# Three later output projections: from one fp32 matmul per chunk to three passes over split operands, weights split in halves

## The reference, cut to what matters

```python
y = jnp.dot(o.reshape(...) * jax.nn.silu(z_x), w_out)      # odd layer: "od_out" in the kernel; x = x + gate * y
x = x + even_mixer_2(rms_norm_2(x, even_norm[i]), ...)      # ends in  o @ w_out            ("e2_out")
x = x + conv_ffn(rms_norm_2(x, ffn_norm[layer]), ...)       # starts with h @ w_up          ("up0", "up1")
x = x + diff_mixer(rms_norm_2(x, odd_norm[i]), ...)         # ends in  o... @ w_out         ("df_out")
```

## Time and profile before

| | |
|---|---|
| median of 3 runs | 2526.52 us (2524.41 to 2529.04) |
| the profiled execution | 2524.14 us, its span 2522.3 us |
| PE busy | 2408.3 us, 95% |
| DVE, ACT, POOL busy | 1147.6, 970.0, 305.8 us (45%, 38%, 12%) |
| DMA | 190.58 MB, mean 76 GB/s |

### The profile page before, as it was taken

How to read it: one execution, slowest core, us unless ns; L and a number is a source line. 1 busy time by engine, 2 the same in 40 slices (tenths; PEclk the granted TensorE clock), 3 DMA queues, 4 the chain that set the end, 5 groups by cost and what they waited for, 6 DMA issues and landing times.

```text
span 2522.3 us, 32773 instructions
## 1 busy us (share of the span) xinstructions
PE 2408.3 (95%) x12528; PEld 1788.9 (71%) x12528; DVE 1147.6 (45%) x1875; ACT 970.0 (38%) x1596; POOL 305.8 (12%) x206
## 2 busy tenths in 40 slices
PE   7999899898999998999999999999999879999998
PEld 4888665466878776665776578888877654888886
DVE  5000454644441106633436356665554452666644
ACT  4111336544254325533325343333342562333423
POOL 2233001200332420000000000004400000000142
PEclk9999799999999999999999999999999999999999
DMA  7122141100231201122220122323322102332331
GB/s 302 53 65 62 67 157 43 58 1 1 74 110 55 80 23 62 51 99 84 77 87 5 42 92 92 98 93 92 100 84 84 42 1 67 96 97 91 93 99 42
DMA packets 51581, 190.58 MB, mean 76 GB/s; under 512 B 5723, under 2 KB 6107, under 8 KB 51196
## 3 DMA queue, kind: packets, MB, share of 16 engines
q1 hardware_dynamic: 51452, 188.78, 23.0%
HBM read 186.66 MB, written 2.10 MB: 75 GB/s over the span
## 4 chain that ended last, share of the span: by engine, by line
PE 89%; ACT 4%; DVE 4%; issue 2%; DMA 0%; POOL 0%; SPq 0%; DVEq 0%; ACTq 0%; POOLq 0%
PE PS L277 7%; PE PS L609 6%; PE PS L607 6%; PE PS L608 6%; PE PS L1656 5%; PE PS L1683 4%; PE PS L2265 3%; PE PS L2264 3%; PE PS L2266 3%; PE PS L1669 3%; PE PS L1363 3%; PE PS L561 3%; PE PS L562 3%; PE PS L560 3%; PE PS L769 2%; PE PS L767 2%
## 5 line engine op out<-in xcount | busy, mean ns | idle before, releaser
L457 POOL TENSOR_TENSOR W_SPLIT<-WT,W_SPLIT 128x1024 fp32r<-128x1024 f32 x44 | 106.9, 2430 | 1452.9 <-ACT W_SPLIT L449 1329.7
L607 PE MATMUL PS<-H_HI,W_SPLIT 128*128 128x512 f32 x672 | 265.5, 395 | 0.0
L609 PE MATMUL PS<-H_HI,W_SPLIT 128*128 128x512 f32 x672 | 265.0, 394 | 0.0
L608 PE MATMUL PS<-H_LO,W_SPLIT 128*128 128x512 f32 x672 | 264.6, 394 | 0.0
L426 ACT ACTIVATE W_SPLIT<-WT 128x1024 fp32r<-128x1024 f32 x84 | 89.0, 1060 | 289.5 <-PE PS L609 267.3
L277 PE MATMUL PS<-SB,WT 128*128 128x512 f32 x384 | 167.3, 598 | 5.2 <-DVE SB L1806 3.1
L2595 DVE TENSOR_TENSOR W_SPLIT<-WT,W_SPLIT 128x1024 fp32r<-128x1024 f32 x80 | 98.0, 1225 | 150.1 <-ACT W_SPLIT L426 150.0
L2580 DVE TENSOR_TENSOR G_LO<-SB,G_HI 128x512 fp32r<-128x512 f32 x44 | 102.8, 2336 | 114.8 <-ACT G_HI L2420 114.8
L608 PEld LDWEIGHTS PS<-H_LO,W_SPLIT 128*128 128x128 f32 x672 | 126.1, 188 | 30.3 <-issue 0.5
L607 PEld LDWEIGHTS PS<-H_HI,W_SPLIT 128*128 128x128 f32 x672 | 126.2, 188 | 29.9 <-issue 0.5
L609 PEld LDWEIGHTS PS<-H_HI,W_SPLIT 128*128 128x128 f32 x672 | 126.3, 188 | 29.7
(11 more groups left out here) (323 smaller groups left out, 5123.0 us busy)
## 6 DMA issues: line engine op xcount, KB each, us to landing
WT<-weights SPq DMA_DIRECT2D x314, 512.0 KB, 3.6
SB<-weights SPq DMA_DIRECT2D x13, 512.0 KB, 12.7
SB<-rpb SPq DMA_DIRECT2D x8, 512.0 KB, 4.4
HT<-rpb SPq DMA_DIRECT2D x8, 512.0 KB, 4.2
XT<-tokens SPq DMA_DIRECT2D x4, 768.0 KB, 6.8
out<-HT SPq DMA_DIRECT2D x4, 512.0 KB, 2.7
SB<-late SPq DMA_DIRECT2D x1, 1280.0 KB, 6.2
SB<-con SPq DMA_DIRECT2D x1, 1248.0 KB
```

The source lines that it names most:

```text
L607: pe.matmul(PS[:, s, :], hi, H_HI[:, c, :], start=(c == 0), stop=False)
L608: pe.matmul(PS[:, s, :], hi, H_LO[:, c, :], start=False, stop=False)
L609: last = pe.matmul(PS[:, s, :], lo, H_HI[:, c, :], start=False, stop=(c == KC - 1))
```

## The change

The three plain output projections are replaced by a class Output with a part for each engine. OUT_HALF holds two halves of a tile, each once, high and low, as W_HALF does for ev_out. The input of the projection is split too, into O_HI (ACT) and O_LO (DVE, over the input itself), before the PE begins; for tile 0 the PE waits for each chunk's O_LO.

```diff
+        class Output:
+            def pe(self, pe):
+                pe.wait_ge(sem("evac_dve"), ev_base[self.name][1])
+                for t in range(8):
+                    for h in range(2):
+                        pe.wait_ge(sem("half_lo"), 2 * (self.half0 + t) + h + 1)
+                        for c in range(4 * h, 4 * h + 4):
+                            if t == 0:
+                                pe.wait_ge(sem("o_lo"), self.lo0 + c + 1)
+                            hi, lo = (OUT_HALF[:, h, k, (c % 4) * 128:(c % 4) * 128 + 128] for k in range(2))
+                            pe.matmul(PS[:, t, :], hi, self.O_HI[:, c, :], start=(c == 0), stop=False)
+                            pe.matmul(PS[:, t, :], hi, self.O_LO[:, c, :], start=False, stop=False)
+                            last = pe.matmul(PS[:, t, :], lo, self.O_HI[:, c, :], start=False, stop=(c == KC - 1))
+                        last.then_inc(sem("tile_used" if h else "half_used"), 1)
+
+            def hi(self, act, t, h):
+                g = self.g0 + t
+                act.wait_ge(sem(f"w_ready{g % SLOTS}"), (g // SLOTS + 1) * 16)
+                if t and h == 0:
+                    act.wait_ge(sem("half_used"), self.used0 + t)
+                elif t:
+                    act.wait_ge(sem("tile_used"), g)
+                act.activation(OUT_HALF[:, h, 0, :], W[:, g % SLOTS, h * 512:h * 512 + 512], ACT.Copy).then_inc(sem("half_hi"), 1)
+
+            def act(self, act):
+                for c in range(KC):
+                    act.wait_ge(sem("at_out"), self.att.b["out"] + c + 1)
+                    act.activation(self.O_HI[:, c, :], self.O[:, c, :], ACT.Copy).then_inc(sem("o_hi"), 1)
+                f0 = FIRST_TILE[self.following]
+                for t in range(8):
+                    if t < 7:
+                        self.hi(act, t + 1, 0)
+                        self.hi(act, t + 1, 1)
+                    late_hi_one(act, self.following, t)
+                    if 1 <= t < 5:
+                        k = t - 1
+                        act.wait_ge(sem(f"w_ready{(f0 + k) % SLOTS}"), ((f0 + k) // SLOTS + 1) * 16)
+                        act.activation(split_of(self.following, k)[:, 0, :], W[:, (f0 + k) % SLOTS, :], ACT.Copy).then_inc(sem("w_hi"), 1)
+
+            def dve(self, v, add):
+                for c in range(KC):
+                    v.wait_ge(sem("o_hi"), self.hi0 + c + 1)
+                    v.tensor_tensor(self.O_LO[:, c, :], self.O[:, c, :], self.O_HI[:, c, :].bitcast(F32), ALU.subtract).then_inc(sem("o_lo"), 1)
+                h0 = split_at[self.following][0]
+                for c in range(KC + 1):
+                    if c < KC:
+                        add(c)
+                    if c >= 1:
+                        v.wait_ge(sem("h_hi"), h0 + c)
+                        v.scalar_tensor_tensor(H_LO[:, c - 1, :], X[:, c - 1, 0:L], gain_late(self.following, c - 1),
+                                               H_HI[:, c - 1, :].bitcast(F32), ALU.mult, ALU.subtract).then_inc(sem("h_lo"), 1)
+                    if 2 <= c < 6:
+                        low_w_dve(v, self.following, c - 2, (FIRST_TILE[self.following] + c - 2) % SLOTS)
+
+            def pool(self, g):
+                for t in range(8):
+                    for h in range(2):
+                        g.wait_ge(sem("half_hi"), 2 * (self.half0 + t) + h + 1)
+                        g.tensor_tensor(OUT_HALF[:, h, 1, :], W[:, (self.g0 + t) % SLOTS, h * 512:h * 512 + 512],
+                                        OUT_HALF[:, h, 0, :].bitcast(F32), ALU.subtract).then_inc(sem("half_lo"), 1)
```

```diff
             def act(self, act, output):
+                    if t == 22:
+                        output.hi(act, 0, 0)
+                        output.hi(act, 0, 1)
...
+            out_od.hi(act, 0, 0)
+            out_od.hi(act, 0, 1)
             att_od.act(act)
+            out_od.act(act)
...
-            project_pe(pe, "od_out", 8, QO, KC, L)
+            out_od.pe(pe)
...
-            project_pe(pe, "e2_out", 8, OFE, KC, L)
+            out_e2.pe(pe)
...
-            low_first("up0")
-            residual_split_dve(v, "up0", residual_one(v, "e2_out", L, None))
+            out_e2.dve(v, residual_one(v, "e2_out", L, None))
```

More of the change, by code:

```diff
@@ L415, in body @@
                 t = 8 * q + s if isinstance(q, int) else None
-                if t == 0:
-                    before(act)
+                if t is not None and t < 4:
+                    return
                 if t == 4:
-                    late_hi_act(act, name)
                     late_squares_act(act, name)
                 act.wait_ge(sem(f"w_ready{slot}"), (rnd + 1) * 16)
[L422 to L426, removed]
+                act.wait_ge(sem("tile_used"), q * 8 + (g0 + s - 1))
+                act.activation(W_SPLIT[:, s % 2, 0, :], W[:, slot, :], ACT.Copy).then_inc(sem("w_hi"), 1)
                 if t == 4:
@@ L798, in pe, with act @@
                         pe.matmul(PS[:, 6 + r % 2, :], std[0], QKE[:, r, :], start=True, stop=True).then_inc(sem("qk_turned"), 1)
[L800 to L804, removed]
+            def act(self, act, output):
+                for t in range(0 if self.early else 4, 26):
+                    if t == 3:
                         late_hi_act(act, self.name)
@@ L858, in turned, with dve @@
                 v.tensor_tensor(x, self.T1[:, r % 2, :], self.T2[:, r % 2, :], ALU.add).then_inc(sem("qk_done"), 1)
-            def dve(self, v, add):
-                for t in range(3 if self.early else 4):
-                    self.low(v, t)
-                residual_split_dve(v, self.name, add)
+            def dve(self, v, add=None):
                 if self.early:
+                    for t in range(3):
+                        self.low(v, t)
+                    residual_split_dve(v, self.name, add)
                     self.low(v, 3)
@@ L888, in values, with __init__ @@
                 eng.wait_ge(sem("v_out"), self.value0 + 8)
+        class Output:
+            def __init__(self, k, name, following, att, hi_at):
+                self.name, self.following, self.att = name, following, att
+                self.g0 = FIRST_TILE[name]
+                self.half0, self.used0 = half_at[name]
+                self.hi0, self.lo0 = 18 + 8 * k, 16 + 8 * k
+                self.O_HI = over(f"O_HI{k}", "SB", BIG + hi_at, [128, KC, L])
+                self.O_LO = over(f"O_LO{k}", "SB", BIG, [128, KC, L])
+                self.O = view(BIG, KC, L)
+            def pe(self, pe):
[53 more added lines that the diff above has]
+                                        OUT_HALF[:, h, 0, :].bitcast(F32), ALU.subtract).then_inc(sem("half_lo"), 1)
@@ L2010, in program @@
                              mask=causal_mask(lambda u: 0), values_in=qkv_df.values, sm_at=PE_AT + 5120, rt_at=PE_AT + 6144, sq_at=PE_AT + 6656, wide=512)
+        OUT_HALF = over("OUT_HALF", "HT", KC * L, [128, 2, 2, TILE // 2])
+        out_od = Output(0, "od_out", "e2_in", att_od, 8192)
+        out_e2 = Output(1, "e2_out", "up0", att_e, 4096)
+        out_df = Output(2, "df_out", "up1", att_df, 4096)
         G = view(BIG, FC, L)
@@ L2283, in _ @@
             att_df.wait(pe)
-            project_pe(pe, "df_out", 8, OFE, KC, L)
+            out_df.pe(pe)
             ffn_pe(1)
@@ L2627, in down_one @@
                 return add
[L2629 to L2634 removed]
+            out_od.dve(v, residual_one(v, "od_out", L, lambda t, b: MOD[:, 40 + t, 0:1]))
+            qkv_e2.dve(v)
             qkv_e2.heads(v)
```

68 lines of the change are left out of this document (37 added, 31 removed).

## The result

| | before | after |
|---|---|---|
| median of the runs, same chip | 2527.78 us (2524.41 to 2529.71, 4 runs) | 2501.26 us (2494.25 to 2504.89, 4 runs) |
| ratio | | 0.9895, interval 0.9879 to 0.9912 |
| the profiled execution | 2524.14 us, its span 2522.3 us | 2504.89 us, its span 2502.7 us |
| PE busy | 2408.3 us, 95% | 2382.7 us, 95% |
| DVE, ACT, POOL busy | 1147.6, 970.0, 305.8 us | 1174.6, 1011.9, 378.3 us |

A forecast was written before the change was run, and what follows sets the result against it. PE, busy for 95% of the span, was taken to bound the kernel. The terms 30.3 - 2.1 - 3.4 - 4.5 - 1.5 gave 18.8 us saved, from the 2526.52 us median to 2507.7 us, range 2498 to 2518 us.

The forecast's parts named there:

- What bounds the kernel: In the three output projections PE alone sets the time; what PE saves ends the kernel earlier if other engines keep up.
- The PE's own work: In each output projection, 192 passes of 0.232 us replace 54.64 us: 10.1 us saved each, 30.3 us in all.
- The rival with faster passes: Projection passes closer than 0.232 us: each 0.01 us less saves 5.8 us more; at the skill's spacing 2498.3 us; chance 2%.
- The start: Each projection's PE starts 0.7 us later, waiting for DVE's first subtraction after its last product: 2.1 us lost in all.
- The clock: Longer PE idling before od_out and e2_out drops the clock to 0.50: 1.7 us lost each, 3.4 us; df_out already pays.
- The halves: In tiles 1 to 6 of each projection, POOL waits for DVE's H_LO, delaying PE 0.25 us each: 4.5 us in all.
- The transfer in od_out: ACT waits for e2_in's first weight tile with the next half queued behind: 1.5 us lost, bounds 0 and 2.2 us.
- POOL loses the port: DVE's 1.22 us weight subtractions go before POOL in four tiles per projection: 14.6 us lost, 2522.3 us; chance 14%, part or whole.
- The attention: The attentions were taken as untouched by the change, the neighbourhood attention's time as before: no gain or cost.
- The sum: Over the whole kernel, 30.3 - 2.1 - 3.4 - 4.5 - 1.5 = 18.8 us saved; chance of this forecast 60%.
- All is hidden: In the projections the clock holds, POOL precedes H_LO, the transfer is early: 28.2 us saved, 2498.3 us; chance 13%.
- Halves that don't fit: ACT and POOL's chain bounds PE at every projection half, 0.93 us each: 16.4 us slower, 2542.9 us; chance 4%.

The follow-up runs named there:

- Experiment 3: Changed kernel with each projection's first three input chunks split before the last attention unit is finished: 2499.28 us, ratio 0.9909 to the kernel before.
- Experiment 5: Changed kernel with both od_out's weight tiles issued early and the first three input chunks split early: 2496.94 us, ratio 0.9885 to the kernel before.
- experiment 8: Kernel before the change, with ACT's table for the exponential loaded ahead of the neighbourhood attention: 2523.98 us, ratio 0.9991 to the kernel before.
- experiment 2: Changed kernel with od_out's tiles 2 to 7 issued during the attention, ahead of later bias tables: 2501.17 us, ratio 0.9907 to the kernel before.
- Experiment 4: Changed kernel with DVE making the following projection's low weights ahead of H_LO: 2507.85 us, ratio 0.9937 to the kernel before.
- the second comparison: The changed kernel run once more without edit against the kernel before: 2502.02 us against 2524.37, ratio 0.9916.

## Why the prediction was right, and where its terms were not

**What bounds the kernel**: right. PE took the gain wherever its operands were there: e2_out at the full clock is 46.1 us, where it was 54.7.

**The PE's own work**, 10.1 us each: nearly right. The spacing is 0.233 us, so 192 passes take 44.8 us and save 9.8 us, 29.5 in all where 30.3 were put. The rival with faster passes is not what the runs show. The Trainium skill (TensorE: Matmul & The Clock Gate, Back-to-back issue gap) gives 216 ns for the isolated gap; the runs have 233 ns.

**The start**, 0.7 us each: 0.82, 2.5 us in all. Experiment 3 took it away, and PE started 0.05 us behind the product again.

**The clock**, 3.4 us: the step that rested on the thinnest reading. It was put on the starts of od_out and e2_out, "because all six cases say so". od_out's start never lost it, in six profiled executions with an idle time of 2.34 us. e2_out's lost it in two of the same six, at 2.38 us. df_out's always lost it at 2.95 us, three times 3.1 us and three times 1.7; of the two with the early inputs, at 2.13 us, one lost it and one didn't. One of the six idle times itself, the 2.02 us in the attention between od_out and e2_out, stands in all ten profiles, and the clock fell behind it in seven. And the idle time of 1.65 us in the neighbourhood attention, one of the five that cost nothing, had a slow clock begin 1.4 to 1.5 us behind it in experiments 5 and 8. In the profile of after the starts cost 0 + 1.7 + 1.4 = 3.1 us more than before, near the 3.4 by luck: one of its two places paid nothing, and df_out, put at nothing more, paid 1.4. What makes the difference is open.

**The halves**, 4.5 us: the mechanism and its timing were right, the size wrong. POOL took 1.74 us where DVE had begun H_LO 0.17 us earlier, and the weight load came 0.24 us late, as forecast (0.25), six times in e2_out and six in df_out, and 0.29 us late in od_out (four times here, six where nothing stalls, in experiment 2). The failed step is the last one, which put the weight load's lateness down as the matmul's. The weight loads run ahead of their matmuls here (at 1418.17 for the matmul at 1418.40), and of 0.24 us only 0.06 came through, of 0.29 us 0.12: with six places in each of the three, 1.5 us in all. Experiment 4 shows the other side of it, 0.70 us late and 0.52 lost. The Trainium skill (GPSIMD Engine Reference, Key points) says that the two engines contend when DVE reads two SBUF inputs; the trace agrees in each of the places read, with 1.73 to 1.80 us for POOL's piece and not 1.30.

**The transfer in od_out**, 1.5 us with 2.2 as the upper bound: the place and the mechanism were right, and the size was off by 4.0 us, the largest error. Experiment 2 measured 5.5 us. That od_out's own tile 2 would be there in time was nearly right: ACT had it 10.2 us behind the last product, where 9.9 were forecast, but without the slow start ACT wanted it 1.83 us sooner, and the PE lost 0.20 us. Four things made the rest. The clock didn't fall at the start, so ACT came to the tile at 1127.9, 17.8 - 3.9 = 13.9 us behind the last product, and waited 3.88 us; the tile itself landed 17.8 us behind it, as before (17.6). The half's copy began only 0.96 us behind ACT's start on the tile. POOL lost its port to DVE's low weights, once, for 1.05 us: what DVE and POOL had to do had piled up behind ACT, and both began at 1133.42. That is the rival "POOL loses the port", in the one place where it came true. And the stall had a slow clock behind it, 1.7 us; that is no rule either, for in experiment 4 a stall of 3.22 us in the same place had none. The upper bound had been the wait alone, and so was none.

**The attention**, at nothing: 1.6 us faster (experiment 8). The prediction had counted the halves of tile 0 as hidden work and hadn't asked what they move. That they moved ACT's load is read from the order of the rows; experiment 8 moved it by hand and got the same stage.

**The sum.** In the profiled execution: 29.5 - 2.5 - 3.1 - 1.5 - 5.5 = 16.9 us against the 17.2 read from the stages. That the forecast of 18.8 comes so near is luck: 3.0 us too much for POOL stand against 4.0 us too little for the transfer. The median's gain of 26.5 us (22.4 in the second comparison) is more than the profiled executions' 19.3, since these lay 3.6 us below and 3.6 us above their medians. The executions of after had mean clocks of 0.983 to 0.987 with times of 2503.74 to 2494.25 us, the profiled one 0.984.

**The rivals.** "All is hidden" fell in all three conditions: the clock fell behind e2_out's start, POOL didn't slip in before H_LO, and the transfer was late. Experiment 5, which comes nearest to it, ran at 2496.9 us. "Halves that don't fit" was right about what the design hangs on, and wrong about this kernel: of 48 POOL pieces, one stalled the matmuls, one cost them 0.20 us, four 0.12 and twelve 0.06. Behind the projections nothing was given back that the clock doesn't explain: from e2_out to df_out it is 618.9 us where it was 617.7, with 1.7 us more of slow clock, and behind df_out 385.2 where it was 385.6.

**What would be better.** Issue the next weights ahead of what isn't wanted soon, and split the first chunks before the last product: 0.9885 against 0.9895 and 0.9916 in the two comparisons of the change as it stands. The stages show it (137.9 us against 147.1 and 148.6), the medians not yet clear of noise.

## What to carry to other kernels

Work woven into a bound engine's stream is worth about its full length (here 15 us of gaps and 6 of slow clock behind them, less the 5.5 of the stall that it brought), but each woven step brings its own input, and the engine's queue makes everything behind it wait for that too: ask of every woven instruction when its transfer lands, not only of those that the stage needs. The bound of such a stall is not the wait but the whole chain behind it, with the port conflicts of work that has piled up and the clock that can fall behind it. A regularity of the clock read from one execution is no rule; run the same kernel twice before a term of the sum rests on it.

## What the runs showed of the hardware

- The same idle time in front of the same stage can or can't bring the clock down to 1.2 GHz: 2.13 us in df_out gave 0.50 in the kernel before and 1.00 in experiment 3; 2.38 us in e2_out gave both in two profiles of one kernel; 2.02 us in the attention before it gave 0.50 in seven of ten profiles; and 3.22 us in od_out (experiment 4) gave 1.00, where 3.76 us had given 0.50. Executions of one kernel range with it from 2499.5 us at a mean clock of 0.985 to 2509.3 at 0.982.
- A weight load that is late by 0.24 us delays the matmuls by 0.06 us; one late by 0.29 us, by 0.12; one late by 0.70 us, by 0.52.
- POOL and DVE, with both inputs in SBUF, all but take turns by whole operations: POOL's 1.30 us became 1.74 beside the rest of a DVE operation of 0.74, 2.20 beside one of 1.22, and 2.35 where both began together.
- A load of ACT's table of functions takes 1.28 us and can stand behind a wait of ACT, where it is paid in full, or ahead of it, where it is hidden.
